# A two-layer decoder on one core: where VectorE's weight splits and TensorE's score products stand in the hand-written order

## The chip, the core and the metric

The kernel runs on one core of a Trainium2 chip. The core has five engines that run side by side: TensorE (PE in the profile, with its weight loads as PEld) multiplies matrices and transposes, VectorE (DVE) and ScalarE (ACT) work elementwise, GpSimd (POOL) does little here, and SyncE (SP) issues the transfers of the weights. Each engine takes its instructions in the order in which the program lists them, and engines wait for each other by semaphores. The metric is the time of one execution in microseconds (us), the median of several runs.

## The reference, cut to what matters

Two layers over 256 tokens (two tiles of 128) with model width 1024. Each layer has three steps, each closed by a residual and a layer norm:

```
x = LN(alpha * x + Mixer(x))          # 6 panels in, 3 kinds of heads, 2 panels out
x = LN(alpha * x + MemXAttn(x, mem))  # q, attention into 256 memory tokens, out
x = LN(alpha * x + FFN_l(x))          # layer 0: dense SwiGLU; layer 1: 8 experts, top 2
```

In the mixer, heads A take two softmax maps each and subtract them,

```
p = softmax(where(causal, q @ k.T * scale, NEG_INF));  a = p[0] - lam * p[1];  o = a @ v
```

heads B are softmax heads with one map that stands for three dilated windows, and heads C are gated linear attention. All is float32 to within a small tolerance.

## The kernel before, in words

**Products.** A weight panel is 1024 x 512 and comes in two halves (128 partitions x 2048 numbers, 1 MB). Most products are made from split operands: a high part, the weight rounded by ScalarE (`split_high`, the cast of line 614, or L633 for the experts), and a low part, what is left, by VectorE (`split_low`, L965, L977). TensorE's `gemm` (L1578) does 24 steps for a panel and a token tile: three products for each of 8 chunks, first high x high, then high x low of the activations, and at steps 8 to 11 and 20 to 23 the products with the low part of the two weight halves. Each takes a 512-column product. The keys and values of the memory attention (`piece`, L1606) are plain float32 products of eight chunks each; TensorE uses them as filler between the small steps of the mixer's attention.

**Order.** All orders are written out by hand, one list for each engine. `split_low(n)` makes VectorE take the next n halves of one fixed list; where the calls stand only decides when. A weight half must be cast by ScalarE before VectorE can split it, and a transfer has to land before that. A ring slot is free for the next transfer when TensorE has used it.

**Mixer's attention.** Seven units u = 0 to 6: four of heads A, three of heads B. For each unit TensorE makes `scores(u)` (L1691); VectorE scales, masks and takes row maxima, `masked_max(u)` (L1064 with L1072 or L1075); ScalarE takes exponentials, `exps(u)` (L699). For u < 4 VectorE then combines two maps, `difference(u)` (L1084 to L1092). TensorE transposes the result, `turn_probs(u)` (L1715), ScalarE copies it out of PSUM, and TensorE multiplies by the values, `values(u)` (L1734). VectorE's list for unit u is: `masked_max(u + 1)`, then `difference(u)`, then side work (decay sums L1141, exponents L1104 and others). ScalarE's list is `exps(u + 1)`, then the copy for unit u. `masked_max(u)` overwrites the buffer that `turn_probs(u - 2)` reads.

**Memory attention.** `cross_output` (L1280, L1283) scales the output of tile t by the softmax sums on VectorE; TensorE transposes it in `turn_xa`.

**Layer norm and turning.** `residual` adds a panel's product to x and takes statistics; `layer_norm` (L926 to L933) needs both panels of a tile. TensorE then transposes the tile (`turn_tile`, L1535), ScalarE writes the high part (`turn_split`, L602) and VectorE the low part (L956); `turned` lets TensorE go on when VectorE is done. The turn between the feed-forward net of layer 0 and layer 1 is called x3, the one ahead of the feed-forward net x2.

**Dense feed-forward net.** Six chunks n of 512 columns (the last has 256). TensorE makes the gate and the up panel, ScalarE the SiLU, VectorE the product `hg` (L1339), TensorE transposes it, ScalarE and VectorE split it (L816, L1353). Then the second matrix follows (`w2`, L1970), which begins when all four accumulation banks have been taken, so after both tiles' `hg` of the last chunk.

Of the kernel before, what the change touches and what calls it, by code (L numbers as in the profile page):

```python
# [146 lines left out]
def bass_decoder(nc, a, out):  # L147
    ctx = ExitStack()
    with ctx:
# [416 lines left out]
        def _(act):  # L566
# [90 lines left out]
            for l in range(DEPTH):  # L657
                for n in range(IN_P):
                    take(l, n, 0, h[:, 0, n * N:(n + 1) * N], h_act)
                    if l == 1 and n == 0:  # L660
                        turn_split(TURN["x3", l - 1], (1,))
# [225 lines left out]
        def _(dve):  # L887
# [128 lines left out]
            for l in range(DEPTH):  # L1016
                lam_init = 0.8 - 0.6 * math.exp(-0.3 * l)
                for n in range(IN_P):
                    if l == 1 and n == 0:
                        layer_norm(2, x, 1)  # L1020
                        split_low(1)
                        turn_split(TURN["x3", l - 1], (1,))
# [275 lines left out]
                split_low(1)  # L1298
# [3 lines left out]
                split_low(1)  # L1302
# [15 lines left out]
                if l == 0:  # L1318
                    layer_norm(3 * l + 1, x, 1)
                    split_low(1)  # L1320
                    turn_split(TURN["x2", l], (1,))
                    split_low(1)
                else:
                    layer_norm(3 * l + 1, x, 1)
                    turn(TURN["x2", l], xT, (1,))
                    low(1, 0)
                if l == 0:
                    for n in range(FFN_CHUNKS + 1):
                        if n < FFN_CHUNKS:
                            w = min(N, F_DENSE - n * N)  # L1330
                            if 0 < n < FFN_CHUNKS - 1:
                                split_low(2)
                            for t in range(T):
# [11 lines left out]
                                if n == FFN_CHUNKS - 1:  # L1345
                                    split_low(1)
# [23 lines left out]
                    split_low(1)  # L1370
# [155 lines left out]
        def _(pe):  # L1526
# [90 lines left out]
            for l in range(DEPTH):  # L1617
                if l == 0:
                    turned(TURN["x0"], 0)
                    gemm_pair(l, 0, 0)  # L1620
                    turned(TURN["x0"], 1)
                else:
                    turned(TURN["x3", l - 1], 0)
                    gemm(l, 0, (0,))
                    gemm(l, 1, (0,), range(20))
                    pe.wait_ge(ln_done, T * 3 * l)
                    turn_tile(TURN["x3", l - 1], x, 1)
                    gemm(l, 1, (0,), range(20, STEPS))
                    turned(TURN["x3", l - 1], 1)
# [109 lines left out]
                piece(l, 0, range(0, 2))  # L1739
                scores(1)  # L1740
                piece(l, 0, range(2, 4))
                for u in range(UNITS):
                    if u == 0:
                        piece(l, 0, range(4, 6))
                    elif u == 1:
                        piece(l, 1, range(0, 2))
                    elif u == 2:
                        piece(l, 1, range(4, 6))
                    elif u == 3:
                        piece(l, 2, range(0, 4))  # L1750
                    elif u == 4:
                        piece(l, 2, range(6, 8))
                        piece(l, 3, range(0, 2))
                    elif u == 5:
                        piece(l, 3, range(4, 7))
                    if u + 2 < UNITS:
                        scores(u + 2)
                    if u == 0:
                        piece(l, 0, range(6, 7))
                    elif u == 1:  # L1760
                        piece(l, 1, range(2, 3))
                    elif u == 2:
                        piece(l, 1, range(6, 7))
                    elif u == 3:
                        piece(l, 2, range(4, 5))
                    elif u == 4:
                        piece(l, 3, range(2, 3))
                    elif u == 5:
                        piece(l, 3, range(7, 8))
# [166 lines left out]
                if l == 0:  # L1936
# [11 lines left out]
                    for n in range(FFN_CHUNKS):  # L1948
                        if n == 0:
                            gemm(l, MIX_PANELS, (0,))  # L1950
                            turn_x("x2", 3 * l + 1, 1)
                            gemm(l, MIX_PANELS + 1, (0,))
# [200 lines left out]
```

## Time and profile before

| | |
|---|---|
| median of 3 runs | 1745.72 us (1744.54 to 1746.57) |
| the profiled execution's own time | 1744.54 us |
| its span, first to last instruction | 1742.7 us |
| mean granted TensorE clock | 0.991 of full speed |
| busy in the span: PE / PEld / DVE / ACT / POOL | 98% / 78% / 76% / 59% / 1% |
| mean HBM traffic | 267 GB/s |

Layer 0 runs from 0 to about 457 us, layer 1 up to the router from there to about 738 us, and the experts from there to the end. In the timeline a row is one instruction or a merged run of them: start, time, engine, line, operation, written tile<-read tiles, count; in square brackets is the idle time ahead of it and what ended that. A 128x512 product of TensorE that is split starts every 0.23 us; its row is longer than that since products overlap. A float32 product counts as two instructions.

### The profile page before, as it was taken

The page shows a single profiled execution, that of the slowest core. Times are in us where ns is not written, and L with a number is a line of the kernel's source. Part 1 is how long each engine was busy: PE and PEld are TensorE (multiplying, and loading weights), DVE is VectorE, ACT ScalarE, POOL GpSimd, SP SyncE. Part 2 cuts the span into 40 slices and gives each one's busy share as a digit, 9 for nine tenths or more (in the row PEclk, how much of TensorE's full clock was granted, in tenths as well). Part 3 has the DMA queues.
Part 4 walks back from the last instruction along what each step waited for, and adds up shares of the span by engine and source line. Part 5 has one row for each costly group of instructions (what it writes and reads, how often), then busy time and mean ns, then how long its engine had stood idle before and what let it go on. Part 6 is the DMA issues. An engine that isn't in the chain of part 4 may idle for free.

```text
span 1742.7 us, 21666 instructions
## 1 busy us (share of the span) xinstructions
PE 1706.1 (98%) x7978; PEld 1364.8 (78%) x7978; DVE 1329.2 (76%) x1226; ACT 1019.6 (59%) x901; POOL 22.1 (1%) x32
## 2 busy tenths in 40 slices
PE   7999999999999999899999999999999999999996
PEld 6856788888785578787888888888888888888885
DVE  4575756545566585689899898898898998998996
ACT  4354344434344444277677777777776776777774
POOL 0001000000000100000000000000000000000000
PEclk9999999999999999899999999999999999999998
DMA  8522436546463242789999999999999999999991
GB/s 301 194 76 76 166 122 212 174 150 231 153 231 105 97 162 104 264 302 355 338 372 371 341 362 370 343 365 353 355 364 357 350 366 339 361 378 338 363 369 64
DMA packets 206487, 465.98 MB, mean 267 GB/s; under 512 B 11968, under 2 KB 14560, under 8 KB 206432
## 3 DMA queue, kind: packets, MB, share of 16 engines
q1 hardware_dynamic: 200896, 463.76, 74.6%
q10 hardware_dynamic: 5536, 1.48, 0.4%
q8 instruction: 36, 0.59, 0.1%
q14 instruction: 19, 0.16, 0.0%
HBM read 464.16 MB, written 1.05 MB: 267 GB/s over the span
## 4 chain that ended last, share of the span: by engine, by line
PE 90%; DVE 6%; DMA 2%; ACT 2%; issue 1%; ACTq 0%; SPq 0%; DVEq 0%
PE ps L1578 20%; PE ps L2053 17%; PE ps L2055 17%; PE ps L2054 17%; PE ps L1606 5%; PE ps L1970 3%; PE ps L2030 2%; PE ps L2039 1%; PE ps L1535 1%; DVE w_lo L977 1%; PE ps L1890 1%; PE ps L1871 1%; DMA ring<-in_w_in_dram 1%; PE ps L1803 1%; PE ps L1734 1%
## 5 line engine op out<-in xcount | busy, mean ns | idle before, releaser
L977 DVE TENSOR_TENSOR w_lo<-ring,w_hi 128x2048 fp32r<-128x2048 f32 x336 | 768.0, 2290 | 112.4 <-ACT w_hi L633 109.4
L633 ACT CAST w_hi<-ring 128x2048 fp32r<-128x2048 f32 x336 | 642.0, 1911 | 277.0 <-PE ps L2055 263.4
L2053 PE MATMUL ps<-w_hi,xe_hi 128*128 128x512 f32 x896 | 353.1, 394 | 1.8 <-DVE w_lo L977 1.8
L2055 PE MATMUL ps<-w_hi,xe_lo 128*128 128x512 f32 x896 | 349.3, 390 | 0.0
L2054 PE MATMUL ps<-w_lo,xe_hi 128*128 128x512 f32 x896 | 348.6, 389 | 0.0
L1578 PE MATMUL ps<-ring_r,xT_r 128*128 128x512 f32 (+1 forms) x760 | 199.4, 392 | 2.8 <-DVE ring_r L965 1.3
L2053 PEld LDWEIGHTS ps<-w_hi,xe_hi 128*128 128x128 f32 x896 | 168.3, 188 | 37.1 <-DVE w_lo L977 2.8
L2055 PEld LDWEIGHTS ps<-w_hi,xe_lo 128*128 128x128 f32 x896 | 168.2, 188 | 35.7
L2054 PEld LDWEIGHTS ps<-w_lo,xe_hi 128*128 128x128 f32 x896 | 168.4, 188 | 33.7
L2053 PE MATMUL ps<-w_hi,he_hi 128*128 128x512 f32 x448 | 178.1, 397 | 0.0
L2055 PE MATMUL ps<-w_hi,he_lo 128*128 128x512 f32 x448 | 174.8, 390 | 0.0
L2054 PE MATMUL ps<-w_lo,he_hi 128*128 128x512 f32 x448 | 174.4, 389 | 0.0
L1578 PEld LDWEIGHTS ps<-ring_r,xT_r 128*128 128x128 f32 x760 | 140.3, 189 | 35.7 <-DVE ring_r L965 1.5
L1606 PE MATMUL ps<-ring,memT 128*128 128x512 f32 x256 | 122.9, 602 | 0.0
L965 DVE TENSOR_TENSOR ring_r<-ring,late_r 128x2048 fp32r<-128x2048 f32 (+1 forms) x36 | 80.0, 2231 | 33.8 <-ACT late_r L614 33.2
L2055 PEld LDWEIGHTS ps<-w_hi,he_lo 128*128 128x128 f32 x448 | 84.1, 188 | 17.9
L2054 PEld LDWEIGHTS ps<-w_lo,he_hi 128*128 128x128 f32 x448 | 84.3, 188 | 16.2
L2053 PEld LDWEIGHTS ps<-w_hi,he_hi 128*128 128x128 f32 x448 | 84.2, 188 | 16.1
L614 ACT CAST late_r<-ring 128x2048 fp32r<-128x2048 f32 (+1 forms) x36 | 66.8, 1862 | 32.2 <-DMA ring<-in_ffd_w_dram 13.5
L965 DVE TENSOR_TENSOR ring_r<-ring,ring_r 128x2048 fp32r<-128x2048 f32 (+1 forms) x28 | 63.0, 2251 | 28.1 <-ACT ring_r L614 27.2
L614 ACT CAST ring_r<-ring 128x2048 fp32r<-128x2048 f32 (+1 forms) x28 | 52.7, 1881 | 41.4 <-DMA ring<-in_w_in_dram 24.3
L1606 PEld LDWEIGHTS ps<-ring,memT 128*128 128x128 f32 x256 | 43.6, 190 | 34.9 <-issue 33.9
(273 smaller groups left out, 1803.2 us busy)
## 6 DMA issues: line engine op xcount, KB each, us to landing
ring<-in_moe_w_dram SPq DMA_DIRECT2D x336, 1024.0 KB, 5.6
ring<-in_ffd_w_dram SPq DMA_DIRECT2D x31, 1024.0 KB, 5.1
ring<-in_w_in_dram SPq DMA_DIRECT2D x24, 1024.0 KB, 6.1
ring<-in_xa_wkv_dram SPq DMA_DIRECT2D x16, 1024.0 KB, 5.0
ring<-in_w_out_dram SPq DMA_DIRECT2D x8, 1024.0 KB, 5.0
ring<-in_xa_wq_dram SPq DMA_DIRECT2D x8, 1024.0 KB, 5.0
ring<-in_xa_wo_dram SPq DMA_DIRECT2D x8, 1024.0 KB, 5.2
ring<-in_ffd_w_dram SPq DMA_DIRECT2D x4, 512.0 KB, 3.6
```

The source lines that it names most:

```text
L614: act.copy(high_half(*name), as_high(raw_half(*name), *name)).then_inc(dense_hi, 1)
L633: act.copy(w_hi[:, q % SPLIT_SLOTS, :], ring[:, q % RAW_SLOTS, :]).then_inc(hi_ready, 1)
L965: dve.tensor_tensor(as_high(low_half(*name), *name), as_high(raw_half(*name), *name), high_half(*name).bitcast(F32), ALU.subtract).then_in ...
L977: dve.tensor_tensor(w_lo[:, q % SPLIT_SLOTS, :], ring[:, q % RAW_SLOTS, :], w_hi[:, q % SPLIT_SLOTS, :].bitcast(F32), ALU.subtract).then_i ...
L1535: ins = pe.transpose(ps[:, 4 + b, c * P:(c + 1) * P], src[:, t, k * P:(k + 1) * P], ident)
L1578: ins = pe.matmul(ps[:, b, 0:w], lhs, weights, start=(step == 0), stop=(step == STEPS - 1))
L1606: ins = pe.matmul(ps[:, piece_bank(i), :], memT[:, k, t * P:(t + 1) * P], raw_half(l, IN_P + n, g)[:, c, :], start=(k == 0), stop=(k == KC ...
L1970: ins = pe.matmul(ps[:, t + 2 * col, :], (h_hi, h_lo)[p][:, k, t * P:(t + 1) * P], weights[q][:, c, col * N:(col + 1) * N], start=(k == 0 ...
L2030: ins = pe.matmul(ps[:, 6 + b, c * P:(c + 1) * P], x[:, t, k * P:(k + 1) * P], sel[:, t, :], start=(t == 0), stop=(t == T - 1))
L2053: pe.matmul(ps[:, bank, :], x_hi, hi[:, c, cols], start=first, stop=False)
L2054: pe.matmul(ps[:, bank, :], x_hi, lo[:, c, cols], start=False, stop=False)
L2055: return pe.matmul(ps[:, bank, :], x_lo, hi[:, c, cols], start=False, stop=last)
```

## The change

Nothing that is computed changes: every product, cast, split and copy is still there once, with the same operands. What changes is where some stand in the lists of TensorE, VectorE and ScalarE. No transfer is moved.

Cut to its core, with the line numbers of the kernel before in the hunk heads:

```diff
@@ -657 ScalarE, layer 1 start @@
-                    if l == 1 and n == 0:
+                    if l == 1 and n == 1:
                         turn_split(TURN["x3", l - 1], (1,))
@@ -1018 VectorE, layer 1 start @@
                         layer_norm(2, x, 1)
-                        split_low(1)
                         turn_split(TURN["x3", l - 1], (1,))
@@ -1295 VectorE, memory attention, both layers @@
                 turn(TURN["q", l], xT, (1,))
-                split_low(1)
+                split_low(2)
                 cross_output(0)
                 turn_split(TURN["xa", l], (0,), xa_lo)
                 cross_max(1)
-                split_low(1)
                 residual(l, o_p, 0, 0)
@@ -1316 VectorE, x2 of layer 0 @@
+                    split_low(2)
                     layer_norm(3 * l + 1, x, 1)
-                    split_low(1)
                     turn_split(TURN["x2", l], (1,))
-                    split_low(1)
@@ -1328 VectorE, dense feed-forward net @@
-                            if 0 < n < FFN_CHUNKS - 1:
+                            if n:
                                 split_low(2)
...
-                                if n == FFN_CHUNKS - 1:
-                                    split_low(1)
@@ -1367 VectorE, end of layer 0 @@
-                    split_low(1)
+                    split_low(2)
@@ -1621 TensorE, layer 1 start @@
-                    gemm(l, 0, (0,))
-                    gemm(l, 1, (0,), range(20))
+                    gemm_pair(l, 0, 0)
                     pe.wait_ge(ln_done, T * 3 * l)
                     turn_tile(TURN["x3", l - 1], x, 1)
-                    gemm(l, 1, (0,), range(20, STEPS))
@@ -1736 TensorE, mixer's attention, both layers @@
                 scores(0)
-                piece(l, 0, range(0, 2))
-                scores(1)
-                piece(l, 0, range(2, 4))
+                piece(l, 0, range(0, 4))
                 for u in range(UNITS):
+                    if u + 1 < UNITS:
+                        scores(u + 1)
...
-                    if u + 2 < UNITS:
-                        scores(u + 2)
@@ -1928 TensorE, x2 of layer 0 @@
                             gemm(l, MIX_PANELS, (0,))
+                            gemm(l, MIX_PANELS + 1, (0,), range(15))
                             turn_x("x2", 3 * l + 1, 1)
-                            gemm(l, MIX_PANELS + 1, (0,))
+                            gemm(l, MIX_PANELS + 1, (0,), range(15, STEPS))
```

Where the attention hunk is cut, the filler pieces are put together: each unit has the same chunks as before (3 ahead of `turn_probs` for u < 3, 5 for u >= 3), but now in one run and not broken by the scores.

TensorE in the first units of the mixer's attention, before, from `scores(1)` (L1691, the 128x256 row) to `values(1)` (L1734, x4). L1606 is a filler chunk, L1715 `turn_probs`, L1660 a transpose of the decays:

```order
L1691 MATMUL ps<-late 128x256 x4
L1606 MATMUL ps<-ring,memT 128x512 x4
L1691 MATMUL ps<-late 128x128 x4
L1606 MATMUL ps<-ring,memT 128x512
L1715 MATMUL ps<-square,late 128x128 x2
L1606 MATMUL ps<-ring,memT 128x512
L1734 MATMUL ps<-h,qk 128x64 x2
L1660 MATMUL ps<-square,cpad 128x128 x4
L1606 MATMUL ps<-ring,memT 128x512 x2
L1691 MATMUL ps<-late 128x256 x4
L1606 MATMUL ps<-ring,memT 128x512
L1715 MATMUL ps<-square,late 128x128 x4
```

The same place now (L1684 is the scores, L1601 a filler chunk, L1708 `turn_probs`, L1727 `values`):

```order
L1684 MATMUL ps<-late 128x256 x4
L1601 MATMUL ps<-ring,memT 128x512 x3
L1708 MATMUL ps<-square,late 128x128 x2
L1601 MATMUL ps<-ring,memT 128x512
L1727 MATMUL ps<-h,qk 128x64 x2
L1653 MATMUL ps<-square,cpad 128x128 x4
L1684 MATMUL ps<-late 128x128 x4
L1601 MATMUL ps<-ring,memT 128x512 x3
L1708 MATMUL ps<-square,late 128x128 x4
```

Before, `scores(2)` stood ahead of `turn_probs(0)`; now it stands behind `values(0)`, at the head of its unit, with three chunks between it and `turn_probs(1)`.

VectorE in the memory attention of layer 0, before, from the copy of the turned q (L912) to the maxima of tile 1 (L1273). L965 is a split, L1280 and L1283 are `cross_output(0)`:

```order
L912 COPY xT<-ps 128x4x128
L965 TENSOR_TENSOR ring_r<-ring,ring_r 128x2048
L1280 RECIPROCAL rsum<-sums 128x4
L1283 TENSOR_TENSOR h<-ps,rsum 128x512 x2
L956 TENSOR_TENSOR late_r<-ps,xT_r 128x512 x2
L1273 TENSOR_REDUCE nmax<-ps 128x4
L1274 TENSOR_SCALAR nmax<-nmax 128x4
L965 TENSOR_TENSOR ring_r<-ring,qk_r 128x2048
```

And now:

```order
L912 COPY xT<-ps 128x4x128
L965 TENSOR_TENSOR ring_r<-ring,ring_r 128x2048
L965 TENSOR_TENSOR ring_r<-ring,qk_r 128x2048
L1279 RECIPROCAL rsum<-sums 128x4
L1282 TENSOR_TENSOR h<-ps,rsum 128x512 x2
L956 TENSOR_TENSOR late_r<-ps,xT_r 128x512 x2
L1272 TENSOR_REDUCE nmax<-ps 128x4
L1273 TENSOR_SCALAR nmax<-nmax 128x4
```

The split that stood behind the maxima of tile 1 now stands ahead of `cross_output(0)`.

VectorE at the end of layer 0, before, from the last split ahead of the layer norm of tile 1 (L926 to L933) to the low part of x3 (L956):

```order
L965 TENSOR_TENSOR ring_r<-ring,late_r 128x2048
L926 BN_AGGR mv<-stats 128x2
L927 TENSOR_SCALAR var<-mv 128x1
L930 SCALAR_TENSOR_TENSOR x<-x,mv,ln_gb 128x1024
L933 SCALAR_TENSOR_TENSOR x<-x,rstd,ln_gb 128x1024
L965 TENSOR_TENSOR ring_r<-ring,late_r 128x2048
L956 TENSOR_TENSOR late_r<-ps,xT_r 128x4x128 x2
```

And now:

```order
L965 TENSOR_TENSOR ring_r<-ring,late_r 128x2048 x2
L926 BN_AGGR mv<-stats 128x2
L927 TENSOR_SCALAR var<-mv 128x1
L930 SCALAR_TENSOR_TENSOR x<-x,mv,ln_gb 128x1024
L933 SCALAR_TENSOR_TENSOR x<-x,rstd,ln_gb 128x1024
L956 TENSOR_TENSOR late_r<-ps,xT_r 128x4x128 x2
```

Both splits now stand ahead of the layer norm; on TensorE the four last steps of the second panel, which need the second of them, have moved from behind the transposes of x3 to ahead of them.

## Rows read from the trace of the kernel before

**Rows 1.** The page: busy time of the engines, and the group of the splits.

```profile
PE 1706.1 (98%) x7978; PEld 1364.8 (78%) x7978; DVE 1329.2 (76%) x1226; ACT 1019.6 (59%) x901; POOL 22.1 (1%) x32
...
L965 DVE TENSOR_TENSOR ring_r<-ring,late_r 128x2048 fp32r<-128x2048 f32 (+1 forms) x36 | 80.0, 2231 | 33.8 <-ACT late_r L614 33.2
```

**Rows 2.** Windows: stretch, length, busy time of each engine, clock, DMA; attention of layer 0.

```profile
88.00:143.00 55.00, 53.72 (x240) 27.90 (x238) 37.01 (x95) 31.97 (x79) 2.61 (x2) 1.00 0.22 77
```

**Rows 3.** Timeline of TensorE in the attention of layer 0, unit 1.

```profile
102.38 0.71 PE L1691 MATMUL ps<-late 32*128 32x256 f32 x8
103.02 1.12 PE L1606 MATMUL ps<-ring,memT 128*128 128x512 f32 x2
103.98 0.60 PE L1715 MATMUL ps<-square,late 128*128 128x128 f32 x4
104.42 1.02 PE L1606 MATMUL ps<-ring,memT 128*128 128x512 f32 x2
105.28 1.08 PE L1734 MATMUL ps<-h,qk 128*128 128x64 f32 x8
```

**Rows 4.** Timeline of VectorE in the same stage, units 1 and 2.

```profile
99.17 0.88 DVE L1064 SCALAR_TENSOR_TENSOR late<-ps,mask_a 128x128 f32<-128x128 f32 x4
...
101.03 0.18 DVE L1084 RECIPROCAL rsum<-sums 128x4 f32<-128x4 f32 x1
...
102.96 1.36 DVE L1141 TENSOR_TENSOR_SCAN qk<-square,late 128x128 f32<-128x128 f32 x4
...
105.57 1.41 DVE L1064 SCALAR_TENSOR_TENSOR late<-ps,mask_a 128x256 f32<-128x256 f32 x4
...
108.49 0.18 DVE L1084 RECIPROCAL rsum<-sums 128x4 f32<-128x4 f32 x1
...
110.02 1.29 DVE L1104 TENSOR_TENSOR late<-qk 128x512 f32<-128x512 f32 x2
```

**Rows 5.** Timeline of three engines in the memory attention of layer 0.

```profile
233.10 1.90 ACT L614 CAST qk_r<-ring 128x2048 fp32r<-128x2048 f32 x1
...
235.47 0.17 DVE L1280 RECIPROCAL rsum<-sums 128x4 f32<-128x4 f32 x1
...
236.56 1.29 DVE L1283 TENSOR_TENSOR h<-ps,rsum 128x512 f32<-128x512 f32 x2 [0.92 <-PE ps L1890]
...
238.01 0.83 PE L1535 MATMUL ps<-square,h 128*128 128x128 f32 x6
...
240.66 1.17 PE L1578 MATMUL ps<-late_r,xT_r 128*128 128x512 f32 x4
```

**Rows 6.** Timeline at x2 of layer 0.

```profile
271.01 0.21 DVE L926 BATCH_NORM_AGGREGATE mv<-stats 128x2 f32<-128x12 f32 x1
...
271.68 1.92 ACT L614 CAST late_r<-ring 128x2048 fp32r<-128x2048 f32 x1 [1.76 <-DMA ring<-in_ffd_w_dram]
...
274.82 1.03 PE L1535 MATMUL ps<-square,x 128*128 128x128 f32 x8
```

**Rows 7.** Timeline at the last feed-forward chunk and the start of `w2`.

```profile
394.79 1.91 ACT L614 CAST qk_r<-ring 128x2048 fp32r<-128x2048 f32 x1 [1.16 <-DMA ring<-in_ffd_w_dram]
...
396.93 0.42 DVE L1339 TENSOR_TENSOR late<-late,ps 128x256 f32<-128x256 f32 x1
...
397.77 0.48 PE L1970 MATMUL ps<-ring_r,h_r 128*128 128x512 f32 x1
```

**Rows 8.** Timeline at x3, tile 1.

```profile
467.51 0.20 DVE L926 BATCH_NORM_AGGREGATE mv<-stats 128x2 f32<-128x12 f32 x1
...
470.78 1.09 PE L1535 MATMUL ps<-square,x 128*128 128x128 f32 x8
...
473.16 1.20 PE L1578 MATMUL ps<-ring_r,xT_r 128*128 128x512 f32 x4 [1.29 <-DVE ring_r L965]
...
474.40 0.47 PE L1578 MATMUL ps<-qk_r,xT_r 128*128 128x512 f32 x1
```

**Rows 9.** Windows, columns as in Rows 2: the router stage of layer 1.

```profile
718.00:736.00 18.00, 11.04 (x52) 10.39 (x52) 11.88 (x25) 2.69 (x3) 0.54 (x1) 0.53 1.04 389
```

More of the change, by code:

```diff
@@ L1738, in _ @@
                 scores(0)
-                piece(l, 0, range(0, 2))
-                scores(1)
-                piece(l, 0, range(2, 4))
+                piece(l, 0, range(0, 4))
                 for u in range(UNITS):
+                    if u + 1 < UNITS:
+                        scores(u + 1)
                     if u == 0:
-                        piece(l, 0, range(4, 6))
+                        piece(l, 0, range(4, 7))
                     elif u == 1:
-                        piece(l, 1, range(0, 2))
+                        piece(l, 1, range(0, 3))
                     elif u == 2:
-                        piece(l, 1, range(4, 6))
+                        piece(l, 1, range(4, 7))
                     elif u == 3:
-                        piece(l, 2, range(0, 4))
+                        piece(l, 2, range(0, 5))
                     elif u == 4:
                         piece(l, 2, range(6, 8))
-                        piece(l, 3, range(0, 2))
+                        piece(l, 3, range(0, 3))
                     elif u == 5:
-                        piece(l, 3, range(4, 7))
-                    if u + 2 < UNITS:
-                        scores(u + 2)
[L1758 to L1769, printed above, removed]
+                        piece(l, 3, range(4, 8))
                         piece(l, 4, range(0, 1))
```

## The prediction

> **What bounds the kernel now.** I read the page's busy times first, then the windows, then the timelines at each place that the change touches. TensorE is busy 1706.1 us of 1742.7, 98% [rows 1]: the reader is to see that there is little wait to take away, 36.6 us in all, 7 of it in the router stage [rows 9], which the change doesn't touch. VectorE is busy 76%, so it has room on average, but what counts is whether a given result is there when TensorE comes for it. In the attention stage, which the largest part of the change rewrites, TensorE is busy 53.72 us of 55 at full clock [rows 2]. So what the change can gain there is at most 1.3 us a layer; what it can lose is open. Since TensorE's products are the same before and after, the change in time is the sum of TensorE's new waits less those that go.
>
> **Mixer's attention, both layers.** The scores of the next unit now stand at the head of a unit. VectorE's list still has the maxima of unit u + 1 ahead of the difference of unit u, and `turn_probs(u)` needs that difference. Before, the scores of u + 1 had been made a unit earlier, and VectorE went on without a wait; now it must wait for scores that TensorE has just made, and TensorE has only three chunks to do meanwhile. I count from the start of the scores at the head of unit u.
>
> The pieces: 128x256 scores take 0.64 us (102.38 to 103.02), a chunk 0.86 (104.42 to 105.28), `turn_probs(1)` 0.44 and `values(1)` at most 1.08 [rows 3]. The narrow maxima of unit 2 take 1.86 (99.17 to 101.03), the difference of unit 1 1.93 (101.03 to 102.96), the wide maxima of unit 3 2.92 (105.57 to 108.49) and the difference of unit 2 1.53 (108.49 to 110.02) [rows 4]. From a difference's last instruction to TensorE's next I take 0.15, from scores to VectorE 0.1, both from the starts that follow each other in these rows.
>
> - u = 0 and u = 2 (wide maxima, narrow difference). VectorE releases at 0.64 + 0.1 + 2.92 + 1.53 + 0.15 = 5.35. TensorE arrives after 0.64 and three chunks with a join, 2.7: at 3.35. It waits 2.0 us, twice.
> - u = 1 (narrow maxima, wide difference). Narrow scores are an estimate at two thirds, 0.43: 0.43 + 0.1 + 1.86 + 1.93 + 0.15 = 4.5 against 0.43 + 2.7 = 3.1. It waits 1.35.
> - u = 3. Five chunks now cover, 4.45; the scores of unit 4, an estimated 0.86, stand on both sides: 5.3. The maxima of unit 4 mix both widths, so lie between 1.86 and 2.92; at 2.4 the release is at 0.86 + 0.1 + 2.4 + 1.93 + 0.15 = 5.45. Wait 0.2 (bounds 0 to 0.7).
> - u = 4 to 6 have no difference; what `values` waits for there is the copy behind the exponentials of the next unit, and five chunks cover its chain of some 0.9 + 2.4 + 2.1. No new wait.
>
> Is VectorE free when the scores come? After the difference of unit 1 it has the decay sums and exponents, 102.96 to 105.57, 2.6 us [rows 4]; TensorE needs 0.44 + 0.86 + 1.08 + 0.64 = 3.0 from `turn_probs(1)` to the end of the next scores [rows 3]. It is, just.
>
> The sum is 2.0 + 1.35 + 2.0 + 0.2 = 5.55 a layer. What goes: half of the 1.28 us of idle time now [rows 2], 0.6, that I put to these units, an estimated 0.3 of smaller gaps, and 0.1 for each of five scores that no longer break a run of chunks (a chunk beside scores takes 0.96, 103.02 to 103.98, and else 0.86 [rows 3]). That leaves 5.55 - 0.9 - 0.5 = 4.15. The level steps behind it are passed hand to hand between TensorE and VectorE and shift as a whole. Both layers: +8.3 us, bounds 7 (joins save twice as much) and 11 (nothing goes).
>
> **Memory attention, both layers.** Two splits now stand ahead of `cross_output(0)`. A split takes 2.2 us [rows 1]. The half of the second is cast by 235.0, so it starts at 235.47 and ends at 237.67. `cross_output(0)` found TensorE's values ready at 236.56 and ran 1.29 us; TensorE took its result at 238.01, straight behind its own work [rows 5]. Now: 237.67 + 0.3 for the reciprocal + 1.3 + 0.15 = 239.4. TensorE waits 1.4. Queued behind the split are `cross_output(0)`, the low part of xa and the maxima of tile 1, which all move by as much; the split that went from behind them leaves only idle time. Two layers: +2.8, bounds 2 and 3.
>
> **x2 of layer 0.** Two splits now stand ahead of the layer norm, from 271.01. The first ends at 273.2. The second needs the cast that starts at 271.68, as its transfer lands, and takes 1.92 [rows 6]: it runs 273.7 to 275.9. A layer norm takes 3.27 from its first instruction to TensorE's transposes (467.51 to 470.78 [rows 8]), so the transposes can start at 279.15. TensorE now has 15 steps of 0.233 from 274.82 to put ahead, to 278.3. It waits 0.85; the nine steps left (2.1 us) cover the casts. +0.85, bounds 0.3 and 1.5.
>
> **Last feed-forward chunk.** Both splits now stand ahead of `hg`. The second one's cast starts at 394.79, again as the transfer lands, and ends at 396.70; the split ends at 398.95. The two `hg` follow, 0.42 each with 0.15 behind, to 400.0. `w2` waits for both. Before, the second `hg` started at 396.93 and `w2` at 397.77, 0.84 later [rows 7]; now the second `hg` starts at 399.5 and `w2` at 400.3. +2.5, bounds 2 and 3. VectorE sits idle 33.8 us ahead of its 36 splits of this kind in all [rows 1], 0.9 us each, so the splits behind it catch up.
>
> **x3.** This edit does take a wait away: the 1.29 us for the low part ahead of the last four steps at 473.16 [rows 8]. What is late next is the layer norm. With a second split ahead of it, it starts at 469.7 and TensorE's transposes at 469.7 + 3.27 = 473.0, against 470.78. The four steps moved ahead fill 0.93 of that, so TensorE is idle 1.35. From the transposes to the next panel's start the casts need 2.65 (the turn of tile 0 in the memory attention took that, 238.01 to 240.66 [rows 5]): 475.65 against 474.40 [rows 8]. +1.25, bounds 0.9 and 1.9.
>
> **The sum.** 8.3 + 2.8 + 0.85 + 2.5 + 1.25 = 15.7 us. Against the profiled execution's own 1744.54 (span 1742.7 and 1.84 around it) this is 1760.2. That execution was the fastest of three, 1.2 below the median of 1745.72, so by the median it is 1761.4. I give 1761. The experts' stage starts from the same state, only later: its first weights are transferred when TensorE frees slots, behind all edits.
>
> **Rivals.**
> *The clock falls.* In the router stage the granted clock was 0.53 on average over 18 us, half speed for nearly all of it, where TensorE's products were small and it was idle for 7 us [rows 9]. At x3 TensorE will do only eight transposes between 471.6 and 475.65, and ahead of `w2` only eight between 396.7 and 400.3. Against it: the 1.29 us wait of now left the clock full, and all stretches of the attention ran at 1.00 [rows 2]. The most that one fall can cost is the half of those 18 us, 8.5 us; since full work follows at once here, I take 2 to 3. With one to three falls: 1763 to 1769.
> The Trainium skill (TensorE: Matmul & The Clock Gate, "HAM oscillation — how this bites in real kernels") says that waits between bursts of products throttle TensorE, and that the burst after the wait runs slowly. It speaks against a change that adds waits of up to 4 us; the trace agrees at the router and shows no fall at waits up to 1.3 us.
> *Only the attention counts.* If VectorE's pairs of splits cost nothing at the four other places, since casts or transfers come earlier than in this trace, the time is 1745.7 + 8.3 = 1754. Against it: at three of them the second split starts behind a cast that waits for its transfer or ends only where I have put it.
> *Not slower.* If VectorE's difference were ready when TensorE arrives, the attention would gain: no score products between chunks, 14 x 0.1 = 1.4, and 1.3 at x3, so with the other splits covered by casts the time would be 1743. The place is `turn_probs(u)` of the first three units, and the point from which it decides is whether maxima and difference (4.45 us together for u = 0) fit into three chunks (2.7 us). They don't in any row here.
>
> **How the numbers follow.** Forecast as summed 0.78, clock falls 0.14, only the attention 0.05, not slower 0.03. The likeliest one's own range is 7 + 2 + 0.3 + 2 + 0.9 = 12.2 to 11 + 3 + 1.5 + 3 + 1.9 = 20.4 above 1745.7, so 1758 to 1766. With the clock's case up to 1768 and a part of the case below, I give 1755 to 1768. A measurement of this kernel can tell about 0.2% from no change, 3.5 us. Faster 0.01, same 0.02 (the third rival), slower 0.97.
>
> **What would show it.** TensorE's waits for VectorE's L1091 (the difference) ahead of `turn_probs`, 2.0, 1.35 and 2.0 us in units 0 to 2 of each layer, and none such from unit 4 on. A wait of 1.4 us ahead of the first turn of xa, once a layer. `w2` starting behind an idle 2.5 us and the x2 transposes behind 0.85. At x3 two waits, 1.35 and 1.8 us, in place of 0.1 and 1.3. The windows over these places at clock 1.00. The prediction is wrong if the attention stage is less than 3 us longer, if the experts' stage gets shorter or longer by more than a us, or if a window at x3 or `w2` shows a clock under 1.

## The result and the profile after

The changed kernel took 1767.76 us (median of 4, 1765.75 to 1768.08), the kernel before 1745.63 beside it (4, 1744.54 to 1746.57). The ratio is 1.0114, 95% interval 1.0101 to 1.0128: slower by 22 us, 1.1%. 1761 was forecast, within 1755 to 1768. The profiled execution took 1769.07 us, its span is 1767.3. A second measurement of the same kernel gave 1765.41 (1763.60 to 1767.60, 4) against 1745.58, ratio 1.0115, interval 1.0100 to 1.0131. With 13 further executions the record has 21 of the changed kernel, 1761.99 to 1768.32 with a median of 1765.49; 48 of the kernel before, taken beside the experiments, lie within 1744.23 to 1746.70. The changed kernel is not only slower, its time also varies 2.5 times as much.

The page, busy time of the engines:

```profile
PE 1711.6 (97%) x7978; PEld 1369.3 (77%) x7978; DVE 1329.5 (75%) x1226; ACT 1020.7 (58%) x901; POOL 22.2 (1%) x32
```

TensorE does the same 7978 products as in [rows 1], but they take 5.5 us longer, and it is idle for 55.7 us against 36.6. So not all of the loss is waiting: some of the products themselves ran slower. TensorE's waits:

```profile
PE ps L1708 <- DVE late L1091: 10.4, 6, 1.9
...
PE ps L1530 <- DVEq L934: 5.3, 4, 3.2
PE ps L1950 <- ACT ring_r L614: 2.7, 1, 2.7
PE ps L1530 <- DVEq L1287: 2.2, 2, 1.1
...
PE ps L1573 <- DVE late_r L956: 1.6, 1, 1.6
```

Each row gives who waited for whom, the us in total, the number of waits and the longest. The first row is the attention's, six waits for the difference, three a layer. The fourth is the memory attention, one a layer. The others are x2 and x3 (with the router's), `w2`, and x3.

**Attention.** TensorE's timeline in layer 0, units 0 to 3, where [rows 3] had no wait:

```profile
100.80 0.44 PE L1708 MATMUL ps<-square,late 128*128 128x128 f32 x2 [1.90 <-DVE late L1091]
...
107.36 0.66 PE L1708 MATMUL ps<-square,late 128*128 128x128 f32 x4 [1.22 <-DVE late L1091]
...
115.11 0.44 PE L1708 MATMUL ps<-square,late 128*128 128x128 f32 x2 [1.89 <-DVE late L1091]
...
116.91 1.66 PE L1684 MATMUL ps<-late 64*128 64x128 f32 x8
```

And VectorE in unit 0, which [rows 4] show for the units behind:

```profile
96.20 1.42 DVE L1063 SCALAR_TENSOR_TENSOR late<-ps,mask_a 128x256 f32<-128x256 f32 x4 [1.27 <-PE ps L1684]
97.77 1.22 DVE L1071 TENSOR_REDUCE nmax<-late 128x4 f32<-128x1024 f32 x1
...
100.13 0.61 DVE L1091 SCALAR_TENSOR_TENSOR late<-late,rsum 128x128 f32<-128x128 f32 x2
```

VectorE now waits for TensorE's scores (1.27 us), makes the maxima, then the difference, and TensorE's `turn_probs` starts 0.06 us behind it: in these units each engine waits for the other once. There is a second thing here. The eight score products from 116.91 take 1.66 us; the same eight take 0.93 in the kernel before (from 115.27), and so do the next eight here (from 125.87). The windows of this stage and of the same one in layer 1:

```profile
90.00:151.00 61.00, 55.29 (x241) 29.73 (x241) 37.07 (x94) 32.63 (x79) 2.61 (x2) 0.97 0.21 70
116.00:118.00 2.00, 2.00 (x13) 1.67 (x12) 0.26 (x1) 0.00 (x0) 0.00 (x0) 0.62 0.20 38
118.00:121.00 3.00, 3.00 (x9) 1.23 (x6) 2.17 (x6) 0.00 (x0) 0.00 (x0) 0.69 0.90 330
...
554.00:613.00 59.00, 52.90 (x233) 27.96 (x232) 36.72 (x94) 31.79 (x78) 2.60 (x2) 1.00 0.22 72
```

From its first product to the first level step the stage took 54.65 us before, in layer 0. Now it takes 60.38 there, with a fall of the clock behind the third wait (0.62 and 0.69 on average over the two windows), and 59.41 in layer 1, at clock 1.00 (54.77 before).

**Memory attention and x2**, layer 0, where [rows 5] and [rows 6] had the start at once:

```profile
242.59 2.29 DVE L965 TENSOR_TENSOR ring_r<-ring,qk_r 128x2048 fp32r<-128x2048 f32 x1
...
244.99 1.29 DVE L1282 TENSOR_TENSOR h<-ps,rsum 128x512 f32<-128x512 f32 x2
246.39 1.09 PE L1530 MATMUL ps<-square,h 128*128 128x128 f32 x8 [1.10 <-DVEq L1287]
...
282.19 2.29 DVE L965 TENSOR_TENSOR ring_r<-ring,late_r 128x2048 fp32r<-128x2048 f32 x1 [0.43 <-ACT late_r L614]
284.40 0.20 DVE L926 BATCH_NORM_AGGREGATE mv<-stats 128x2 f32<-128x12 f32 x1
...
287.66 1.09 PE L1530 MATMUL ps<-square,x 128*128 128x128 f32 x8 [0.74 <-DVEq L934]
```

The split stands ahead of what TensorE needs, and TensorE waits 1.10 and 0.74 us. From the turn of q to the first product of the next panel the memory attention took 9.13 us before and 10.45 now, +1.3 in each layer.

**The start of `w2`** ([rows 7]), timeline:

```profile
406.11 2.29 DVE L965 TENSOR_TENSOR ring_r<-ring,qk_r 128x2048 fp32r<-128x2048 f32 x1 [0.76 <-ACT qk_r L614]
...
408.99 0.42 DVE L1336 TENSOR_TENSOR late<-late,ps 128x256 f32<-128x256 f32 x1 [0.25 <-DVE late L1336]
...
409.83 1.03 PE L1950 MATMUL ps<-ring_r,h_r 128*128 128x512 f32 x2 [2.73 <-ACT ring_r L614]
```

The row names a cast of ScalarE (407.65 to 409.56). But `w2` starts 0.84 us behind the start of the second `hg`, exactly as in [rows 7], where the same cast came behind the start of `w2` (398.26): what it waits for is `hg`.

**x3** ([rows 8]), timeline, and the windows behind both places:

```profile
483.51 0.20 DVE L926 BATCH_NORM_AGGREGATE mv<-stats 128x2 f32<-128x12 f32 x1
...
486.78 1.09 PE L1530 MATMUL ps<-square,x 128*128 128x128 f32 x8 [1.18 <-DVEq L934]
...
489.48 2.04 PE L1573 MATMUL ps<-qk_r,xT_r 128*128 128x512 f32 x4 [1.61 <-DVE late_r L956]
```

```profile
410.00:413.00 3.00, 3.00 (x8) 2.31 (x8) 3.00 (x4) 1.83 (x1) 0.00 (x0) 0.50 0.77 306
488.00:490.00 2.00, 0.52 (x1) 0.50 (x2) 1.29 (x2) 2.00 (x3) 0.00 (x0) 0.63 0.00 0
490.00:492.00 2.00, 2.00 (x6) 1.57 (x5) 0.00 (x0) 0.34 (x1) 0.00 (x0) 0.50 0.00 0
492.00:496.00 4.00, 4.00 (x12) 3.10 (x12) 0.00 (x0) 0.00 (x0) 0.00 (x0) 0.58 0.01 1
```

The waits are where they were forecast. Behind both the clock is down for several us: two `w2` products take 1.03 us and took 0.71 before, and four panel steps 2.04 against 1.20 in [rows 8].

The difference step by step, read between the same TensorE products in both traces, in us:

| step | forecast | this profile | second profile | alone (its profile) |
|---|---|---|---|---|
| before the attention, code not changed | 0 | +1.7 | +0.7 | |
| attention, layer 0 | +4.15 | +5.7 (fall) | +4.45 | +5.7 (fall) |
| memory attention, layer 0 | +1.4 | +1.3 | +1.3 | +1.3 |
| x2 | +0.85 | +0.95 | +1.15 | +1.05 |
| last chunk and `w2` | +2.5 | +4.2 (fall) | +4.2 (fall) | +2.65 |
| x3 | +1.25 | +4.1 (fall) | +2.4 (fall) | +1.3 |
| attention, layer 1 | +4.15 | +4.65 | +4.65 | +4.45 |
| memory attention, layer 1 | +1.4 | +1.3 | +1.3 | +1.3 |
| router, gather and experts, code not changed | 0 | +0.7 | +0.6 | |

"Alone" is the profile of the kernel with that edit by itself, in the experiments below. Stages whose code is the same differ too: over the profiles of the experiments the start is 0.1 to 1.7 us longer than in the one profile of the kernel before (1.5 and 1.7 in two kernels that don't touch the attention), and the router stage with its gather, where its waits are not filled, from 0.2 shorter to 1.1 longer.

### The profile page after: what moved, and what is told of

Its sections match the earlier page's. It is cut to its first block, busy times and chain, and to the rows that moved or that the text cites. A ratio compares the mean times of both kernels' runs of the same rounds, so it can differ in the third digit from the quotient of the medians.

```text
span 1767.3 us, 21667 instructions
## 1 busy us (share of the span) xinstructions
PE 1711.6 (97%) x7978; PEld 1369.3 (77%) x7978; DVE 1329.5 (75%) x1226; ACT 1020.7 (58%) x901; POOL 22.2 (1%) x32
## 3 DMA queue, kind: packets, MB, share of 16 engines
HBM read 464.16 MB, written 1.05 MB: 263 GB/s over the span
## 4 chain that ended last, share of the span: by engine, by line
PE 87%; DVE 6%; DMA 2%; ACT 2%; ACTq 1%; issue 1%; SPq 0%; DVEq 0%
PE ps L1573 18%; PE ps L2033 17%; PE ps L2035 17%; PE ps L2034 17%; PE ps L1601 5%; PE ps L1950 3%; PE ps L2010 2%; PE ps L1530 1%; PE ps L2019 1%; DVE ring_r L965 1%; DMA ring<-in_w_in_dram 1%; DVE w_lo L977 1%; PE ps L1727 1%; PE ps L1782 1%; PE ps L1684 1%
## 5 line engine op out<-in xcount | busy, mean ns | idle before, releaser
L1601 PE MATMUL ps<-ring,memT 128*128 128x512 f32 x256 | 121.5, 603 | 0.0
L965 DVE TENSOR_TENSOR ring_r<-ring,late_r 128x2048 fp32r<-128x2048 f32 (+1 forms) x36 | 79.8, 2230 | 33.3 <-ACT late_r L614 32.6
L965 DVE TENSOR_TENSOR ring_r<-ring,ring_r 128x2048 fp32r<-128x2048 f32 (+1 forms) x28 | 63.0, 2251 | 36.0 <-ACT ring_r L614 35.4
L1601 PEld LDWEIGHTS ps<-ring,memT 128*128 128x128 f32 x256 | 44.7, 192 | 40.3 <-issue 39.3
```

Of the source, the lines that this page charges most:

```text
L965: dve.tensor_tensor(as_high(low_half(*name), *name), as_high(raw_half(*name), *name), high_half(*name).bitcast(F32), ALU.subtract).then_in ...
L1601: ins = pe.matmul(ps[:, piece_bank(i), :], memT[:, k, t * P:(t + 1) * P], raw_half(l, IN_P + n, g)[:, c, :], start=(k == 0), stop=(k == KC ...
```

## The experiments

The expectation of each is quoted as it was written before the run; "A" and "B" are defined in each.

**The attention alone.** The kernel before, with only TensorE's new order in the mixer's attention:

```
                 scores(0)
-                piece(l, 0, range(0, 2))
-                scores(1)
-                piece(l, 0, range(2, 4))
+                piece(l, 0, range(0, 4))
                 for u in range(UNITS):
+                    if u + 1 < UNITS:
+                        scores(u + 1)
...
-                    if u + 2 < UNITS:
-                        scores(u + 2)
```

> The kernel before with the attention hunk alone (TensorE's scores at the head of each unit). Theory A (VectorE's difference is late, 2.0 + 1.35 + 2.0 us a layer): TensorE waits about 10.4 us in six waits for the difference; attention stages together +8.3 to 9 us, and +1.5 more for each fall of TensorE's clock in them; time 1754 to 1757. Rival B (most of the change's cost lies in the splits of VectorE and the clock at x3 and w2): 1748 or less.

Measured: 1754.70 us (1753.88 to 1755.45, 4) against 1745.25, ratio 1.0055, interval 1.0038 to 1.0071: +9.45. Its windows in layer 0:

```profile
88.00:149.00 61.00, 55.31 (x242) 29.85 (x240) 37.32 (x95) 32.58 (x79) 2.60 (x2) 0.97 0.20 70
...
116.00:118.00 2.00, 2.00 (x8) 0.83 (x6) 1.00 (x4) 0.00 (x0) 0.00 (x0) 0.50 0.90 307
```

The attention's edit by itself makes both its waits (10.2 us over six, 10.4 in the whole change) and its fall of the clock, at the same unit. The time is within the 1754 to 1757 of theory A.

**The waits filled.** The changed kernel, with products of constants on TensorE in its new waits. Nothing reads their results.

```
+            def warm(count, bank):
+                for _ in range(count):
+                    pe.matmul(ps[:, bank, 256:512], ...wr_hi, ...wr_split, start=True, stop=True)
...
+                    if u < 3:                       # ahead of turn_probs(u)
...
+                        warm((15, 9, 15)[u], 2 + u % 2)
...
+                    warm(22, 6)                     # ahead of w2
...
+                    warm(9, 4)                      # ahead of the turn of x3
                     turn_tile(TURN["x3", l - 1], x, 1)
+                    warm(13, 4)                     # behind it
```

> The changed kernel with extra 128x256 products of constants, results never read, on TensorE ahead of its five kinds of new wait (15, 9, 15 in attention units 0 to 2, 22 ahead of w2, 9 and 13 at x3): the waits on VectorE stay as they are, but TensorE is busy in them. Theory A (the three falls of the clock, ahead of unit 3 of layer 0, at w2 and at x3, cost 1.5 + 1.5 + 2.7 = 5.8 us): the clock is 1.00 in all three places and the time 1762, give or take 1. Rival B (the time goes to the waits alone, the clock in these rows costs nothing that the waits would not cost): no change or slower, 1768 to 1769.

Measured: 1762.43 us (1760.71 to 1763.26, 4), ratio 1.0097, interval 1.0080 to 1.0114. Windows over the places:

```profile
88.00:143.00 55.00, 54.07 (x260) 31.25 (x259) 36.78 (x94) 30.25 (x75) 2.60 (x2) 1.00 0.24 77
400.00:416.00 16.00, 15.86 (x101) 14.07 (x100) 13.98 (x11) 9.79 (x9) 0.00 (x0) 1.00 0.70 236
470.00:500.00 30.00, 29.92 (x143) 24.60 (x142) 20.87 (x18) 11.71 (x10) 0.54 (x1) 1.00 0.51 175
536.00:591.00 55.00, 53.96 (x289) 34.30 (x287) 32.12 (x81) 24.12 (x68) 0.95 (x1) 1.00 0.25 83
```

The waits for VectorE are as long as they were, only filled (the attention of layer 0 is 4.45 us longer than before, as in the second profile), and in this profile the clock stays at 1.00 in all of these places. That takes 5.3 us off the first measurement of the changed kernel, 3.0 off the second and 3.1 off the median of all 21. What is left is 17.2 us: 16.6 of it are the changed stages in the table at full clock, the price of the waits, and the rest is of the size by which unchanged stages differ.

**The difference ahead of the maxima.** The attention alone, as above, and VectorE makes the difference of unit u before the maxima of unit u + 1:

```
                 for u in range(UNITS):
+                    if u < 4:
+                        difference(u)
                     if u + 1 < UNITS:
                         masked_max(u + 1)
-                    if u < 4:
-                        difference(u)
```

> As e1, and in VectorE's list the difference of unit u stands ahead of the maxima of unit u + 1. Theory A (the difference is late only because it is queued behind maxima that wait for scores just made): no wait of TensorE for the difference is left; what is late next is ScalarE's copy, behind the exponentials of unit u + 1: TensorE's values of units 0 and 2 wait 1.7 us for it, unit 1 0.3, in all 3.7 a layer against 5.5, so 3 to 4 us faster than e1. Rival B (the difference itself or ScalarE's exponentials of unit u are late, wherever it stands): the waits for the difference stay at 1.2 to 1.9 and the time is that of e1.

Measured: 1756.47 us (1752.35 to 1758.31, 4), ratio 1.0062, interval 1.0045 to 1.0078, no gain on 1754.70, where 3 to 4 us were expected. TensorE's waits, and its windows in layer 1:

```profile
PE ps L1734 <- ACT qk L715: 7.5, 4, 2.2
```

```profile
88.00:146.00 58.00, 53.41 (x240) 28.62 (x237) 37.97 (x96) 31.43 (x79) 2.60 (x2) 1.00 0.23 77
...
555.00:560.00 5.00, 5.00 (x17) 2.45 (x16) 4.66 (x13) 2.24 (x9) 0.00 (x0) 0.74 0.00 0
...
565.00:570.00 5.00, 3.59 (x15) 2.16 (x16) 3.99 (x13) 1.36 (x7) 0.00 (x0) 0.79 0.58 210
```

`turn_probs` no longer waits, but `values` does, for the copy that ScalarE can make only when the maxima have given it the next exponentials: 7.5 us over four waits in place of 10.2 over six, as theory A had it. The stage in layer 0 was shorter as expected (57.74 us, against 59.1 to 59.2 without a fall), but layer 1 had two falls and took 60.66. The first of them came behind a single wait, 2.20 us at 552.22; in layer 0 a wait of 2.21 us at the same place had none. So the same order was run without them:

**The same with the waits filled.** 17 and 13 products of constants, not read, ahead of `values(0)` and `values(2)`:

```
+                    if u in (0, 2):
...
+                        warm((17, 0, 13)[u], 3)
```

> As e3, with extra 128x256 products of constants, results never read, on TensorE in its waits ahead of values(0) and values(2) (17 and 13). Theory A (e3 lost in layer 1 to falls of the clock what it gained in layer 0): the clock is 1.00 through both attention stages, both last 57.7 us from the decay product to the first level product, 3.1 more than before, and the time is 1751 to 1752. Rival B (the swapped order itself costs, above all in layer 1, in waits for ScalarE's copy): stages of 60 us and the time of e3, 1755 to 1757.

Measured: 1751.15 us (1750.45 to 1752.32, 7) against 1745.75, ratio 1.0033, interval 1.0021 to 1.0044.

```profile
88.00:146.00 58.00, 56.97 (x269) 32.48 (x268) 37.63 (x95) 31.45 (x80) 2.60 (x2) 1.00 0.22 73
540.00:598.00 58.00, 57.03 (x276) 32.64 (x276) 36.29 (x93) 32.08 (x79) 2.59 (x2) 1.00 0.22 73
```

Both stages now take 57.7 us, as theory A had it. The filled kernel is 5.3 us faster; 3.0 of that is the stage in layer 1 with its falls gone, and of the rest the two profiles show 1.9 in the start and the router stage, whose code is the same. And even with the falls gone and VectorE in its better order, the new order of scores costs 3 us a layer (54.65 and 54.77 before), against 4.45 with the difference behind the maxima. The chain from scores over maxima and exponentials to ScalarE's copy still ends later than three chunks do.

**The last feed-forward chunk alone:**

```
-                            if 0 < n < FFN_CHUNKS - 1:
+                            if n:
                                 split_low(2)
...
-                                if n == FFN_CHUNKS - 1:
-                                    split_low(1)
```

> The kernel before with the feed-forward hunk alone (in the last chunk both splits ahead of hg). Theory A (w2 waits 2.5 to 2.7 us more for hg, which stands behind a split whose cast waits for a transfer, and the clock falls behind that wait for about 1.5 us more): from the transposes of chunk 4 to those of chunk 5 the trace shows 8.2 us in place of 4.0, and the time is 4 us longer, 1749 to 1750. Rival B (the wait comes but the clock stays full, its fall in the changed kernel being a matter of chance): 2.6 longer, 1748. Rival C (the cost came from the shift of the stages ahead): 1746 or less.

Measured: 1749.10 us (1748.50 to 1750.76, 10) against 1745.75, ratio 1.0020, interval 1.0011 to 1.0030: +3.35. TensorE's timeline at the start of `w2` and the window:

```profile
401.56 0.71 PE L1968 MATMUL ps<-ring_r,h_r 128*128 128x512 f32 x2 [2.72 <-ACT ring_r L614]
```

```profile
401.00:404.00 3.00, 2.44 (x11) 2.02 (x12) 2.85 (x4) 0.69 (x2) 0.00 (x0) 1.00 0.87 321
```

The wait is the same as in the changed kernel (2.72 against 2.73 us), yet here no fall follows: the two products behind it take 0.71, not 1.03. The time is that of theory A, the trace that of rival B: the stage is 2.65 us longer. Where the other 0.7 of the median comes from isn't shown; the start of this profile is 1.5 us longer than that of the kernel before, with the same code.

**x3 alone:**

```
-                    if l == 1 and n == 0:
+                    if l == 1 and n == 1:
                         turn_split(TURN["x3", l - 1], (1,))
...
-                    split_low(1)
+                    split_low(2)
...
-                    gemm(l, 0, (0,))
-                    gemm(l, 1, (0,), range(20))
+                    gemm_pair(l, 0, 0)
...
-                    gemm(l, 1, (0,), range(20, STEPS))
```

> The kernel before with the edits at x3 alone (second split ahead of the layer norm, four steps ahead of the transposes). Theory A (the layer norm is late by a split: two waits of 1.2 to 1.35 and 1.6 to 1.8 us, in all 1.3 us longer, and the clock falls behind the second, 2.7 more): 1749 to 1750. Rival B (no fall): 1746.5 to 1747. Rival C (the wait of 1.3 us that goes outweighs the late layer norm): 1744.5 or less.

Measured: 1747.56 us (1746.43 to 1749.92, 10), against 1745.75, ratio 1.0011, interval 1.0001 to 1.0020: +1.8.

```profile
474.69 1.09 PE L1534 MATMUL ps<-square,x 128*128 128x128 f32 x8 [1.17 <-DVEq L934]
477.39 1.17 PE L1577 MATMUL ps<-qk_r,xT_r 128*128 128x512 f32 x4 [1.61 <-DVE late_r L956]
```

Again both waits as in the changed kernel, and no fall: four steps behind them take 1.17 us, where they took 2.04. The stage is 1.3 us longer, as rival B had it, and the median is half a us above rival B's range. One of the ten executions took 1749.92 us, with the lowest mean clock of them, 0.989 against 0.991 to 0.993.

**Memory attention and x2 alone**, the splits ahead of `cross_output(0)` and of the layer norm:

```
-                split_low(1)
+                split_low(2)
                 cross_output(0)
...
                 cross_max(1)
-                split_low(1)
...
+                    split_low(2)
                     layer_norm(3 * l + 1, x, 1)
-                    split_low(1)
                     turn_split(TURN["x2", l], (1,))
-                    split_low(1)
...
+                            gemm(l, MIX_PANELS + 1, (0,), range(15))
                             turn_x("x2", 3 * l + 1, 1)
-                            gemm(l, MIX_PANELS + 1, (0,))
+                            gemm(l, MIX_PANELS + 1, (0,), range(15, STEPS))
```

> The kernel before with the edits in the memory attention and at x2 alone. Theory A (cross_output is late by 1.3 us in each layer, the x2 layer norm by 0.8 to 1.0, the clock stays full since the waits are short): +3.5 us, 1748.5 to 1749. Rival B (later slack takes them up): 1746.

Measured: 1749.41 us (1748.69 to 1749.99, 10), against 1745.75, ratio 1.0022, interval 1.0012 to 1.0031: +3.65, as summed in the prediction (1.4, 1.4 and 0.85) and as its profile has it (1.3, 1.3 and 1.05).

**All but the attention**, the changed kernel with TensorE's order in the attention put back, and **the changed kernel once more**:

> The changed kernel with only the mixer's attention put back as it was: all edits outside the attention together. The question is whether the parts add up. A (they add up, each costs what it costs alone): x3, w2 and the memory attention with x2 were 1.8, 3.35 and 3.7 us each by itself, so 8.85 together: 1754.6 us, clock 1.00 at w2 and at x3. B (the falls of the clock at w2 and x3, 1.5 and 2.7 us in the changed kernel's profile, belong to these edits when they stand together, whatever the attention does): 8.85 + 4.2 = 13: 1758 to 1759, with clock 0.5 to 0.7 behind the waits at w2 and at x3. C (the falls there come with the place in time that the attention's waits shift): as A.

> The changed kernel once more, unaltered, on the same chip as the one beside it. A (falls of the clock are settled by the order of the work and come back at the same waits): 1766 to 1768 us, with the clock of the first profile, 0.6 to 0.7 in units 3 and 4 of layer 0's attention, 0.5 behind the wait at w2 and 0.5 to 0.6 behind those at x3. B (a fall is a matter of one execution): the profile shows them at other places, and the time of each fall that is missing, 1.5 to 2.7 us, is off the span of 1767.3.

Measured: 1755.71 us (1753.86 to 1758.06, 5) without the attention's edit, against 1745.58, ratio 1.0061, interval 1.0047 to 1.0074; the changed kernel as given at the top. First the kernel without the attention's edit, TensorE at `w2` and x3:

```profile
402.32 0.70 PE L1964 MATMUL ps<-ring_r,h_r 128*128 128x512 f32 x2 [2.58 <-ACT ring_r L614]
...
477.50 1.09 PE L1530 MATMUL ps<-square,x 128*128 128x128 f32 x8 [1.14 <-DVEq L934]
480.21 2.05 PE L1573 MATMUL ps<-qk_r,xT_r 128*128 128x512 f32 x4 [1.61 <-DVE late_r L956]
```

Then the second profile of the changed kernel, the third wait of layer 0's attention and windows:

```profile
114.13 0.44 PE L1708 MATMUL ps<-square,late 128*128 128x128 f32 x2 [1.89 <-DVE late L1091]
...
89.00:149.00 60.00, 54.21 (x247) 29.03 (x247) 37.06 (x94) 32.83 (x80) 2.60 (x2) 1.00 0.21 71
...
408.00:410.00 2.00, 2.00 (x6) 1.59 (x5) 2.00 (x3) 1.06 (x1) 0.00 (x0) 0.50 0.95 379
...
488.00:490.00 2.00, 2.00 (x7) 1.56 (x6) 0.00 (x0) 0.00 (x0) 0.00 (x0) 0.56 0.00 0
```

Without the attention's edit there is no fall at `w2` but one at x3, 1.4 us. In the second profile of the changed kernel the waits of layer 0's attention are 1.89, 1.23 and 1.89 us, as in the first, and the clock stayed at 1.00 throughout; `w2` fell again, and the fall at x3 cost 1.3 us in place of 2.7 (from its first product behind the wait to the seventeenth, 5.09 and 6.47 against 3.80 at full clock). The span was 4 us shorter, 1763.3, of which 1.0 is the start. So neither A nor B of either expectation holds in full: the waits come back in each execution to within 0.2 us, the falls behind them don't. A wait makes a fall possible; whether it comes, and how long it lasts, differs between two executions of one program. Over the four profiles that have the edit unfilled, `w2` fell in two and x3 in three, and the attention of layer 0 in two of its three; that `w2` fell in both profiles with the attention's edit and in neither without it is too few to tell a rule from chance.

The parts nearly add up: 9.45 + 3.35 + 1.8 + 3.65 = 18.3 us by themselves, 9.45 + 10.1 = 19.6 by halves, 19.8 and 22.1 for the whole in its two measurements. The whole has the more falls.

**The router's waits filled.** [rows 9] show the one place between its first and its last microseconds where the kernel before itself runs at half clock. The kernel before, with 26, 12, 16 and 8 products of constants, not read, in TensorE's waits there:

```
+                    warm(26, 5)      # ahead of the transposes of x
...
+                    warm(12, 5)      # ahead of the second tile's router products
...
+                    warm(16, 5)      # ahead of the counts
...
+            warm(8, 4)               # ahead of the gather
```

> The kernel before with extra 128x256 products of constants, results never read, in TensorE's waits of the router stage (26 ahead of the last turn, 12, 16 and 8 behind). If TensorE's clock follows how busy it is, the router stage (0.53 over 718 to 736 us) runs at full clock, its transposes take 0.9 in place of 2.0 us, the router products 1.8 in place of 3.6 and the gather 3.5 in place of 5.6: 3 to 5 us faster, 1741 to 1743. If the fall does not depend on the wait: as before or 1 us slower.

Measured: 1740.94 us (1740.05 to 1741.72, 8) against 1745.25, ratio 0.9973, interval 0.9962 to 0.9984. It is the only kernel here that beats the one before.

```profile
718.00:736.00 18.00, 17.79 (x145) 17.18 (x145) 14.35 (x29) 4.06 (x6) 0.54 (x1) 1.00 1.04 388
```

The 4.3 us gained are within the 3 to 5 expected. The clock is at 1.00 in place of 0.53; the eight transposes of x take 1.09 us, and took 1.97 before.

## Why the prediction was right, and which step failed

**How right.** The terms as summed are right: they gave 15.7 us, and with the waits filled, so at full clock, the kernel takes 17.2 more than before. The point forecast of 1761 is 6.8 us below the first measurement and 4.4 below the second, and what is missing is mostly the falls of the clock. The first measurement lies 0.2 us inside the stated range and above the 1758 to 1766 of the case that was given 0.78; that it is inside is in part luck. By the prediction's own list of signs it is wrong at one: a window at x3 and at `w2` shows a clock under 1.

**What bounds the kernel.** Right in part: the loss is TensorE's new waits. That the change in time is nothing but these waits, since the products are the same, is not right: the same 7978 products are busy 5.5 us longer. The start of the kernel, whose code is the same, added 1.7 us in the first profile and 0.7 in the second, for the most part in a wait for a cast (1.52 and 0.60 us); why it differs is not explained, but it differs as much between kernels with other edits, so it does not belong to this change.

**Attention.** The waits came at `turn_probs` of units 0, 1 and 2 with 1.90, 1.22 and 1.89 us where 2.0, 1.35 and 2.0 were worked out, and none where 0.2 was. The term that was mis-sized is what goes in return: 1.4 us a layer was taken off (0.9 for idle time and small gaps, 0.5 for unbroken chunks), and at full clock 5.0 us of waits made the stage 4.45 longer, so it was 0.55. The two errors partly cancel: 4.15 forecast, 4.45 and 4.65 measured at clock 1.00.

**Memory attention, x2, `w2`, x3.** All four waits came from the split put ahead of what TensorE needs, as told. At full clock they cost 1.3 a layer, 1.0, 2.65 and 1.3 us, against 1.4, 0.85, 2.5 and 1.25. The experts' stage, the gather and the router together kept their length to within 0.7 us.

**The step that failed** is the weight of the rival "the clock falls". Without it the terms as measured sum to about 16.6 us, against 15.7. With it come three falls in the profile: 1.3 us in the attention (60.4 less 59.1, the stage at full clock), 1.5 at `w2` (4.2 less 2.65) and 2.7 at x3. Their sum is the 5.5 us of busy time. The rival had the number (one to three) right; its price of 2 to 3 us holds for x3 and is too high for the other two. Its time, 1763 to 1769, holds both measurements; but it was given 0.14, and the point estimate was taken without it. The argument against it was that a wait of 1.29 us left the clock full in the kernel before. That wait too stands behind eight transposes (from 470.78), like the one at `w2`, but the new ones are longer, 2.73 us at `w2`, or come together: 1.18 and 1.61 around the transposes of x3, and three of 1.2 to 1.9 in 16 us in the attention. Apart from its start, the kernel before waited longer than 1.3 us in two places, and both showed a fall: the router, and one place near the end of the kernel, which the prediction does not mention:

```profile
1728.18 0.50 PE L2068 MATMUL ps<-y_hi,backT 128*128 128x512 f32 x1 [2.00 <-DVE y_lo L1465]
```

And the window behind it:

```profile
1728.00:1732.00 4.00, 2.82 (x8) 1.72 (x8) 2.96 (x6) 0.13 (x1) 0.00 (x0) 0.67 0.00 0
```

Behind this wait of 2.00 us the products start every 0.23 us at first and every 0.43 from 1729.52 on. That filled waits kept the clock at 1.00 at all these places in the profiles, and made the kernel faster, is shown; its times also spread less (1760.71 to 1763.26 over four executions, and 1750.45 to 1752.32 with the difference first, where that kernel unfilled took 1752.35 to 1758.31); what decides whether a given execution has the fall stays open.

**Other rivals.** "Only the attention counts" is refuted by the runs of the other parts, +3.35, +1.8 and +3.65 by themselves. "Not slower" is refuted by the waits at `turn_probs`; even with the difference moved ahead of the maxima a wait, of up to 2.2 us, appears at `values`.

## What to carry to other kernels

When an edit moves work so that a busy engine waits, the sum of its waits is not the whole price: look for places in the trace where waits of 1 to 3 us stand close together or next to small products, and forecast those twice, at full and at half clock. Here about half of them fell in any one profile, at 1.3 to 2.7 us each. Where TensorE must wait in such a place, products of constants that nobody reads can be cheaper than idling, if they end by the time that what it waits for is there. And when one engine's list is reordered, check the other engine's list for a result that now has to be made within a single unit, since swapping two steps there can move much of the wait to the next consumer: here 10.2 us of waits became 7.5.

## What the hardware showed that was not expected

- The clock fell already behind waits of 1.90, 1.22 and 1.89 us within 16 us (0.62 on average over 116 to 118 us), behind one of 2.20 us (0.74 over 555 to 560 us of the kernel with the difference first), and behind 1.18 and 1.61 us with eight transposes between them, to 0.50, the lower level of 1.2 GHz.
- The same waits, within 0.02 us, were followed by a fall in one execution and by none in another: of the same program in the attention (1.90, 1.22 and 1.89 with, 1.89, 1.23 and 1.89 without), and of programs with the same code there at `w2` (2.73 with, 2.72 without) and x3 (1.18 and 1.61 with, 1.17 and 1.61 without). By the windows a fall lasted from 3 to 7 us, and it cost 1.3 to 2.7.
- Filling four waits in the router stage of the kernel before, which changes none of its results, gained 4.3 us of 1745.
